# A chunked recurrent block on TensorE: shared operands in matmuls of 128 columns, and diagonal pairs as 128x128 weights

## The reference, cut to what matters

```python
def step(state, inp):
    r_t, w_t, k_t, v_t, a_t, b_t = inp
    sa = jnp.einsum('bhij,bhj->bhi', state, a_t)
    state = (state * w_t[:, :, None, :] + sa[..., None] * b_t[:, :, None, :]
             + v_t[..., None] * k_t[:, :, None, :])
    return state, jnp.einsum('bhij,bhj->bhi', state, r_t)
xs = tuple(jnp.moveaxis(t, 1, 0) for t in (r, decay, k, v, a_vec, b_vec))
_, ys = lax.scan(step, jnp.zeros((B, H, N, N), jnp.float32), xs)
```

## Time and profile before

| what | value |
|---|---|
| three runs | 1958.47, 1959.4 and 1967.14 us, median 1959.4 |
| span of the profiled execution | 1958.9 us |
| PE busy | 1641.4 us, 84% of the span |
| VectorE, ScalarE, POOL busy | 676.9, 370.8, 195.1 us |
| DMA | 537.14 MB, mean 274 GB/s |

### The profile page before, as it was taken

One profiled execution on the slowest core, in us unless ns is written; L12 is line 12 of the kernel. 1 busy time (PEld: TensorE's weight loads), 2 busy tenths in 40 slices (PEclk: granted clock), 3 DMA queues, 4 the chain that ended last, 5 costly groups with the idle time before them and its releaser, 6 DMA issues.

```text
span 1958.9 us, 30727 instructions
## 1 busy us (share of the span) xinstructions
PE 1641.4 (84%) x13306; PEld 1041.2 (53%) x13306; DVE 676.9 (35%) x1148; ACT 370.8 (19%) x746; POOL 195.1 (10%) x91
## 2 busy tenths in 40 slices
PE   9999999999999998766676787999988768666664
PEld 8998977997985854222122332867854223221221
DVE  1565421564531365111111124573365211111103
ACT  1444101444201251000000011331211000000001
POOL 2331422331420000000000000000300000000000
PEclk9999999999999999888878898999999989888888
DMA  9342444351453448999999997222156999999994
GB/s 383 106 165 97 162 159 172 100 171 44 190 213 156 172 185 351 427 427 427 427 427 427 425 388 315 105 86 72 64 238 281 427 426 425 426 428 427 427 427 192
DMA packets 48231, 537.14 MB, mean 274 GB/s; under 512 B 4533, under 2 KB 12981, under 8 KB 15033
## 3 DMA queue, kind: packets, MB, share of 16 engines
q1 hardware_dynamic: 46752, 528.27, 65.9%
q10 hardware_dynamic: 1304, 6.51, 0.9%
HBM read 533.71 MB, written 1.05 MB: 273 GB/s over the span
## 4 chain that ended last, share of the span: by engine, by line
PE 59%; DMA 31%; DVE 5%; ACT 3%; issue 1%; POOL 0%; DVEq 0%; ACTq 0%; POOLq 0%
PE ps L448 47%; DMA arena<-in_moe_w_gu 23%; PE ps L460 8%; DMA arena<-in_moe_w_down 6%; PE ps L466 2%; DMA ring<-in_moe_w_gu 2%; DVE x L1539 1%; ACT arena L2421 1%; DVE arena L1528 1%; ACT arena L2425 1%; DVE arena L1533 1%; DVE arena L1539 1%; ACT L2421 0%; DVE hb L1528 0%; DVE small L1543 0%
## 5 line engine op out<-in xcount | busy, mean ns | idle before, releaser
L460 PE MATMUL ps<-arena 128*32 128x512 f32 (+1 forms) x1348 | 201.6, 680 | 86.0 <-DMA arena<-in_moe_w_gu 66.4
L448 PE MATMUL ps<-hT,ring 128*128 128x256 f32 (+2 forms) x1600 | 265.5, 326 | 0.0
L2425 ACT ACTIVATE arena<-ps 128x512 f32<-128x512 f32 (+4 forms) x152 | 92.4, 608 | 898.8 <-PE ps L460 491.5
L460 PE MATMUL ps<-ring,arena 128*32 128x512 f32 x1248 | 178.6, 703 | 89.9 <-DMA ring<-in_moe_w_gu 71.9
L448 PEld LDWEIGHTS ps<-hT,ring 128*128 128x128 f32 (+1 forms) x1600 | 236.4, 186 | 25.1 <-issue 2.1
L1528 DVE TENSOR_TENSOR arena<-arena,ps 128x256 f32<-128x256 f32 (+3 forms) x110 | 55.6, 506 | 486.5 <-ACT arena L2421 432.8
L448 PE MATMUL ps<-arena 64*64 64x64 f32 (+11 forms) x2000 | 149.7, 302 | 30.8 <-ACT arena L2714 22.3
L460 PEld LDWEIGHTS ps<-arena 128*32 128x32 f32 (+1 forms) x1348 | 48.8, 124 | 221.6 <-DMA arena<-in_moe_w_gu 98.2
L460 PEld LDWEIGHTS ps<-ring,arena 128*32 128x32 f32 x1248 | 38.2, 120 | 205.2 <-DMA ring<-in_moe_w_gu 102.1
L448 PEld LDWEIGHTS ps<-arena 64*64 64x64 f32 (+4 forms) x2000 | 92.2, 150 | 86.4 <-ACT arena L2714 49.5
L448 PE MATMUL ps<-arena,ring 128*128 128x256 f32 (+2 forms) x928 | 129.6, 315 | 2.8 <-ACT hT L2425 1.4
(11 more groups left out here) (205 smaller groups left out, 1824.5 us busy)
## 6 DMA issues: line engine op xcount, KB each, us to landing
arena<-in_moe_w_gu SPq DMA_DIRECT2D x57, 2048.0 KB, 40.9
ring<-in_moe_w_gu SPq DMA_DIRECT2D x49, 2048.0 KB, 41.2
ring<-in_moe_w_down SPq DMA_DIRECT2D x35, 2048.0 KB, 41.3
arena<-in_moe_w_down SPq DMA_DIRECT2D x29, 2048.0 KB, 40.7
extra<-in_moe_w_gu SPq DMA_DIRECT2D x22, 2048.0 KB, 41.5
ring<-in_w_merge SPq DMA_DIRECT2D x16, 2048.0 KB, 8.3
ring<-in_w_in SPq DMA_DIRECT2D x9, 2048.0 KB, 7.3
ring<-in_attn_w_qkv SPq DMA_DIRECT2D x6, 2048.0 KB, 7.7
```

Source lines behind the costliest of these rows:

```text
L448: i = t.matmul(o, l, r, start=first, stop=last, skip_group_check=True)
L460: i = t.matmul(o, l, r, start=first, stop=last, skip_group_check=True)
L2425: s.activation(o, a, ACT.Copy).then_inc(*act.one(name))
```

## The change

`with_both` takes the place of four `pair` calls per block: the operands r and a lie beside each other (`r.ra`), so one matmul of 128 columns with b as weights gives rb and N, and one with k gives rk and ak. Its results fill two PSUM tiles, one for each partition half of the operands. U and W come from one matmul of 128 columns (`mv atok` holds both right sides), in two half tiles `UW0` and `UW1`; H and R likewise (`rb btok`), one tile for each chunk. The six Horner updates use weights of 128x128, with chunk 0's matrix in the upper left quarter, chunk 1's in the lower right and zeros elsewhere: 16 matmuls of 128x128 by 64 columns instead of 32 of 64x64 by 64 columns. To lay the weights so, ScalarE copies the first eight heads of pw1 and of Q twice, scaled by 1 and 0 over the partitions (`first_half`), and VectorE writes the other eight in one operation (`other_half`). `mv`, `ktok` and `btok` are moved between the updates. Memory is dealt out anew.

```diff
+    r.ra = arena[:, OWN + 4096:OWN + 8192].rearrange("p (t k s) -> p t k s", t=2, k=KT)
...
-        def quads(i, n, lhs, rhs, out, order=None):
+        def with_both(i, n, lhs):
             name = f"rw{i} {n}"
+            p = [tile(f"{name}{a}", (dve, f"{name}{a} out")) for a in range(2)]
+            mm([(p[a][64 * c:64 * c + 64, P * k:P * k + P], lhs[64 * a:64 * a + 64, k, i * P + 64 * c:i * P + 64 * c + 64],
+                 r.ra[64 * a:64 * a + 64, :, k, i * P + 64 * c:i * P + 64 * c + 64], True, True)
+                for k in range(KT) for c in range(2) for a in range(2)], name)
...
+        def step(n, rhs, last, power=None):
+            for i in range(NT):
...
+                mm([(p[:, 64 * b:64 * b + 64], B[i]["P"][:, P * b:P * b + P], B[i][rhs][:, 64 * b:64 * b + 64], True, True)
+                    for b in range(16)], name)
...
-        def summed(left, n, step):
-            for i in range(NT):
-                if step > 1:
-                    t.wait_ge(*dve(f"rw{i} {n}{step - 1} out"))
-                quads(i, f"{n}{step}", B[i][left], B[i]["X" if step > 1 else "Y"], dve)
...
-            pair(i, "N", r.bT, r.aa)
+            with_both(i, "N", r.bT)
             pair(i, "D", r.aa, r.bT)
-        values(1)
+            if i == 0:
+                values(1)
...
-        summed("d", "R", 1)
-        for i in range(NT):
-            pair(i, "rb", r.bT, r.rT)
-        summed("d", "R", 2)
-        for i in range(NT):
-            pair(i, "rk", r.kT, r.rT)
-        summed("d", "R", 3)
+        values_of_keys(0)
+        step("R1", "Y", "inv1", "pw1")
+        with_both(1, "K", r.kT)
+        step("R2", "X", "R1")
+        values_of_keys(1)
+        step("R3", "X", "R2")
+        t.wait_ge(*act("rw0 mv out"))
+        tokens(0, "ktok", r.kT)
...
+        t.wait_ge(*act("rw1 mv out"))
+        tokens(1, "ktok", r.kT)
+        step("P1", "Y", "R3", "Q")
+        tokens(0, "btok", r.bT)
+        step("P2", "X", "P1")
+        tokens(1, "btok", r.bT)
+        step("P3", "X", "P2")
...
-            quads(i, "U", B[i]["Y"], B[i]["mv"], act, (at_, lambda u: u, lambda u: u))
...
+                mm([(p[64 * c:64 * c + 64, P * (u % 8):P * (u % 8) + P], blk_of(B[i]["Y"], c, at_(u)),
+                     B[i]["mv atok"][64 * c:64 * c + 64, u], True, True) for u in range(8 * j, 8 * j + 8) for c in range(2)], name)
...
-            mm([(p[onto(u, c)], blk_of(d["W"], c, u), blk_of(d["btok"], c, u), True, True) for u, c in uc], name)
+            for n, c in ((c + 1, c) for c in range(2)):
+                w = 64 if i and c else P
+                mm([(p[c][64 * (u % 2):64 * (u % 2) + 64, P * (u // 2):P * (u // 2) + w], blk_of(d["W"], c, u),
+                     d["rb btok"][64 * c:64 * c + 64, 0:w // 64, 64 * u:64 * u + 64], True, True) for u in range(16)], f"rw{i} RH{c}")
...
+        def inverse_starts(i):
...
+            v.wait_ge(*pe(f"rw{i} N"))
+            for a in range(2):
+                masked(heads(d["n"], a), half_of(i, "N", a, 1), "m16", f"rw{i} n" if a else None)
+            v.wait_ge(*pe(f"rw{i} D"))
+            masked(u3(d["d"]), u3(ps(f"rw{i} D")), "n16", f"rw{i} D out")
+            for a in range(2):
+                masked(heads(d["Dm"], a), half_of(i, "N", a, 1), "mof")
+                masked(rb[:, a], half_of(i, "N", a, 0), "mle", f"rw{i} N{a} out")
...
+        def other_half(i, n):
+            v.wait_ge(*pe(f"rw{i} {n}"))
+            tt(B[i]["full"][:, 8:16], bc(u3(ps(f"rw{i} {n}"))[:, 8:16].unsqueeze(2), [P, 8, 2, 64]),
+               bc(tab["hnd"].unsqueeze(1).unsqueeze(3), [P, 8, 2, 64]), MUL, f"rw{i} {n} other")
...
+        def first_half(i, n):
+            s.wait_ge(*pe(f"rw{i} {n}"))
+            for c in range(2):
+                fn(B[i]["full"][:, 0:8, c], u3(ps(f"rw{i} {n}"))[:, 0:8], ACT.Copy, f"rw{i} {n} out" if c else None, scale=m.tab["hnd"][:, c:c + 1])
...
-    for q, step in enumerate(("rw1 ak", "rw1 mv", "rw1 rb", "rw1 rk")):
+    for q, step in enumerate(("rw0 K", "rw0 mv", "rw1 K", "rw1 mv")):
```

More of the change, by code:

```diff
@@ L430, in memory @@
     r.bT, r.aa = r.aT, r.kk
+    r.ra = arena[:, OWN + 4096:OWN + 8192].rearrange("p (t k s) -> p t k s", t=2, k=KT)
+    r.rb_btok = [arena[:, o:o + 2048].rearrange("p (t x) -> p t x", t=2) for o in (OWN + 2048, OWN + 13312)]
     r.add = [flat(r.kT)[:, 1024 * i:1024 * i + 1024] for i in range(NT)]
@@ L1359, in rwkv @@
             t.wait_ge(*dve(f"rw{i} D out"))
-            quads(i, "sq n", B[i]["d"], B[i]["n"], act)
-            quads(i, "sq d", B[i]["n"], B[i]["d"], act)
-        for i in range(NT):
-            pair(i, "ak", r.kT, r.aa)
+            quads(i, "sq n", B[i]["d"], B[i]["n"], (act, f"rw{i} sq n out"))
+            quads(i, "sq d", B[i]["n"], B[i]["d"], (act, f"rw{i} sq d out"))
+        with_both(0, "K", r.kT)
         for i in range(NT):
@@ L1366, in rwkv @@
             t.wait_ge(*pool(f"rw{i} Y"))
-            quads(i, "inv1", B[i]["d"], B[i]["Y"], dve)
-            quads(i, "pw1", B[i]["n"], B[i]["d"], act)
+            quads(i, "inv1", B[i]["d"], B[i]["Y"], (dve, f"rw{i} inv1 out"))
+            quads(i, "pw1", B[i]["n"], B[i]["d"], (act, f"rw{i} pw1 out"), (dve, f"rw{i} pw1 other"))
         t.wait_ge(*act("rw v1"))
-        for i in range(NT):
[L1371 to L1375, removed]
-        summed("d", "R", 1)
-        for i in range(NT):
-            pair(i, "rb", r.bT, r.rT)
-        summed("d", "R", 2)
-        for i in range(NT):
-            pair(i, "rk", r.kT, r.rT)
-        summed("d", "R", 3)
-        for i in range(NT):
-            t.wait_ge(*act(f"rw{i} mv out"))
-            tokens(i, "ktok", r.kT)
+        values_of_keys(0)
[6 more added lines that the diff above has]
+        tokens(0, "ktok", r.kT)
         for i in range(NT):
@@ L1392, in rwkv @@
             t.wait_ge(*act(f"rw{i} X0 out"))
[L1393 to L1400, removed]
+            quads(i, "Q", B[i]["Dm"], B[i]["X"], (act, f"rw{i} Q out"), (dve, f"rw{i} Q other"))
+        t.wait_ge(*act("rw1 mv out"))
[5 more added lines that the diff above has]
+        step("P3", "X", "P2")
         for i in range(NT):
             t.wait_ge(*dve(f"rw{i} P3 out"))
-            t.wait_ge(*act(f"rw{i} btok"))
-            quads(i, "U", B[i]["Y"], B[i]["mv"], act, (at_, lambda u: u, lambda u: u))
[L1405 to L1408, removed]
+            t.wait_ge(*act(f"rw{i} atok"))
+            for j in range(2):
+                name = f"rw{i} UW{j}"
+                p = tile(name, (act, f"rw{i} UW{j} a"), (dve, f"rw{i} UW{j} b"))
+                mm([(p[64 * c:64 * c + 64, P * (u % 8):P * (u % 8) + P], blk_of(B[i]["Y"], c, at_(u)),
+                     B[i]["mv atok"][64 * c:64 * c + 64, u], True, True) for u in range(8 * j, 8 * j + 8) for c in range(2)], name)
         def onto(u, c):
@@ L1472, in rwkv @@
         scan(1)
-        reads(1)
         scan(2)
@@ L1502, in blocks @@
         slot = m.ring[m.spare[i]]
[L1503 to L1506, removed]
+        d = {"P": slot[:, 0:2048], "Dm": slot[:, 2048:3072], "rk": slot[:, 3072:4096], "Q": flat(m.mT if i else r.Lc),
+             "rb": r.own[3 * i], "btok": r.own[3 * i + 1], "ak": r.own[3 * i + 2], "rb btok": r.rb_btok[i],
+             "mv atok": (flat(m.hT) if i else m.hb.rearrange("p t d -> p (t d)")).rearrange("p (u t n) -> p u t n", u=16, t=2)}
+        for pair, names in (("P", "nd"), ("Q", "YX")):
             for k in range(2):
                 d[names[k]] = d[pair][:, 1024 * k:1024 * k + 1024]
-        d["U"], d["W"], d["H"], d["G"] = d["n"], d["d"], d["E"], d["X"]
-        d["atok"], d["btok"], d["ktok"] = d["Nm"], d["Dm"], d["ak"]
+        d["UW"] = d["P"].rearrange("p (t u n) -> p t u n", t=2, u=16)
+        d["full"] = d["P"].rearrange("p (b c n) -> p b c n", b=16, c=2)
+        d["U"], d["W"], d["H"], d["G"] = d["n"], d["d"], d["Dm"], d["X"]
+        d["ktok"] = d["ak"]
         B.append(d)
@@ L2305, in rwkv @@
            ps("rw bonT")[:, 0:512].rearrange("p (g q n) -> p g q n", g=4, q=4)[:, :, :, 0:2], "rw bonT")
-        for i in range(NT):
-            masked(i, "ak", ("ak", "mlt"))
+        keys_read(0)
         for i in range(NT):
@@ L2367, in reads @@
         def reads(i):
[L2369 to L2371 removed]
+            for c in range(2):
+                v.wait_ge(*pe(f"rw{i} RH{c}"))
+                rt = rT[:, :, i * P + 64 * c:i * P + 64 * c + 64]
+                tt(rt, rt, read_or_gained(i, c, 0), ADD, f"rw{i} R{c}")
         def seen(i, rows):
@@ L2871, in rwkv @@
             out(i, "sq d", B[i]["d"])
+        def first_half(i, n):
+            s.wait_ge(*pe(f"rw{i} {n}"))
+            for c in range(2):
+                fn(B[i]["full"][:, 0:8, c], u3(ps(f"rw{i} {n}"))[:, 0:8], ACT.Copy, f"rw{i} {n} out" if c else None, scale=m.tab["hnd"][:, c:c + 1])
         for i in range(NT):
-            out(i, "pw1", B[i]["d"])
+            first_half(i, "pw1")
         for i in range(NT):
-            out(i, "mv", B[i]["mv"])
-        for i in range(NT):
-            out(i, "ktok", B[i]["ktok"], "")
```

(13 more changed lines are left out.)

97 lines of the change are left out of this document (57 added, 40 removed).

## The result

The changed kernel takes 1977.14 us, the median of five runs from 1973.44 to 1979.52, beside 1959.4 for the kernel before, also of five. The ratio of the two is 1.0077 (95% interval 1.0057 to 1.0097): slower, by more than the half per cent that can be told from no change. The profiled execution has a span of 1976.0 us, 17.1 more than before.

The account below looks back on a forecast made before the run. PE's in-order list was taken to bound the block, its growth delaying the DMA-bound weight stream and the end one for one. Terms summed to +17.2 us on 1958.9, giving 1976.1, as median 1976.5; eight-in-ten range 1967 to 1985.5 us.

Parts of the forecast that it names:

- U with W: Four merged half tiles of 32 records at 1.95 us each against 4 x 1.87: +0.3 us; range -3.7 to +7.8.
- Horner steps: Twelve R and P updates with full 128x128 weights cost 3.62 us each instead of 1.87: +21.0 us.
- rival that the load hides: Horner steps: weight load hides behind the matmul ahead, a step costs 1.87 us; about 1955.5 us; chance 0.12.
- Stops that go: PE's nine unexplained issue stops in the block, 10.0 us with restarts, mostly vanish as streams slow: -9.0 us.
- rival by which they stay: PE's stops in the block come from instruction supply and remain: +9.0 us more, about 1985.5 us; chance 0.10.
- Merged pair products: N with rb, ak with rk: eight products become four of 128 columns at 1.95 us: -0.3 us.
- rival of two at a time: Merged pair products overlap by two instead of four, 3.9 us each: +7.5 us, about 1984 us; chance 0.10.
- H with R: Merged per chunk, only two array quarters work instead of four: 6.8 us against 4.0, +2.8 us.
- The wait for a PSUM tile: Block 1's first squaring waits for VectorE to free one of N's two PSUM tiles: +2.7 us.
- The ScalarE wait: PE's wait ahead of P1 goes, since block 1's `ktok` fills it and VectorE takes half of Q: -1.2 us.
- The scan's cover: Block 1's R no longer stands between scan1 and the VectorE wait, leaving 1.6 us bare for 1.34: +0.3 us.
- rival that it absorbs it: After the block, the expert weight stream absorbs the block's delay: 1959.5 us; chance 0.04.

Follow-up runs that it names:

- e1: Changed kernel with its twelve Horner products back to 32 matmuls of 64x64 by 64 columns, all else kept; 1956.18 us, ratio to before 0.9984.
- e2: Changed kernel with each Horner matmul cut into two of 32 moving columns, same 128x128 weights, so twice the loads; 2092.72 us (one run).
- e3: Changed kernel with each Horner matmul cut by output into two with weights of 128 rows by 64 columns; 1957.9 us, ratio 0.9995.
- e4: Kernel before, with the matmuls inside each pair product reordered so that two quarters of the array work at a time, not four; 1970.35 us (one run).
- e7: Changed kernel with Horner products back on quarters and VectorE and scan reordered to shorten both new PE waits; 1953.55 us, ratio to before 0.9972.
- e5: Changed kernel with VectorE reordered to finish each half of N at once and free its PSUM tile early; 1971.02 us, ratio 1.0062.
- e6: Changed kernel with scan1 ahead of block 1's G as cover, and VectorE reading R before writing the state; 1973.16 us, ratio 1.0064.

## Why the prediction held

The forecast of 1976.5 us is 0.6 off the median, and the main term is shown: e1, e2 and e3 settle that a full-array step is paid for by its weight loads. Some terms beside it missed and cancelled: that the sum came within 1 us is luck, that it lies near 17 us isn't. (Two slips in it hardly matter: 1976.1 + 0.5 is 1976.6, and U with W without overlap would be +8.1, not +7.8.)

- **Horner steps**, predicted +21.0: twelve take 43.15 us from start to start, less 12 x 1.87 = +20.7. The 0.6 for switches between full-array and quarter products isn't seen apart from it; taken together it was 21.6 for 20.7. The rival that the load hides is refuted by the profile after, and e1 undoes the loss.
- **Stops that go**, predicted -9.0: 0.6 us are left, with the restart 0.8, so -9.2. The size was right, the reason only in part. The prediction laid the stops to the 16 ns rate alone and gave instruction supply to the rival by which they stay. But e4's pair products at 25 ns leave 6.3 us of them, and e7's squarings, which run at 29 ns a record, have a stop of 1.49 us. The traces put every stop at a block of PE's own instruction list (last section): supply is the cause they point to, and a slower list is why the stops went. e1 says which part did it: with steps in quarters 1.9 us are left, so most went with the merged products.
- **Merged pair products**, predicted -0.3: 1.83 us (2.84 to the transposes less 1.01 for D) for each N, 1.91 and 1.86 for the two of K, 7.43 for 8.08: -0.65. The rival of two at a time would have read 3.9 each.
- **U with W**, predicted +0.3: 6.82 us (1423.24 to 1430.06) for 4 x 1.87: -0.7. **H with R**, predicted +2.8: 2.91 (1430.06 to 1432.97) and 2.14, together 5.05 for 4.0: +1.1. Both terms were mis-sized by the same step: I took 0.122 us for two matmul records that share the array, from a row of four side by side; 6.82 us over 64 such pairs is 0.107, and 2.91 us over the 32 pairs of block 0's H with R is 0.091.
- **The wait for a PSUM tile**, predicted +2.7: 2.89, and e5 shows its cause. **The ScalarE wait** ahead of P1 is gone, -1.2 as predicted.
- **The scan's cover**, predicted +0.3: the wait is 2.37 for 1.34, +1.0. I took 1.6 us, VectorE's two operations with hand-overs. I missed that scan2 takes the PSUM tile of RH0, which VectorE reads only behind the state, from 1447.32 on and for 0.7 us; PE goes on at 1448.06, and the profile names that read (`arena`) as the releaser and not the state (`cz`). In e6, where the read comes first, the wait is 0.79.
- **The clock**, not in the sum: the squarings take 8.92 us where four products of 1.87 make 7.48 (+1.4), and the scan with the last chunk product about 1.5 us more than in e1 and e5. The windows say 0.81 and 0.61. The prediction took 1.00 for the whole block, as before.

20.7 - 9.2 - 0.65 - 0.7 + 1.1 + 2.9 - 1.2 + 1.0 + 2.9 = +16.85, beside the measured 16.94. Of the errors, the clock and the scan are 3.6 us that the sum lacked; U, W, H and R are 2.7 that it had too many, the switches, pairs and steps the rest.

The stream behind the block took the delay as predicted; the rival that it absorbs it is refuted by its first chunk at 1454.53. The prediction gave near 1456; the block began 1.2 us earlier than before.

## What to carry to other kernels

Two 64x64 weight matrices laid as one block-diagonal 128x128 halve the instructions and double the time where few columns move: the halves can no longer be loaded beside each other. Before packing, look in the trace for the packed shape at the same column count and read its start-to-start distance; counting instructions would have given the wrong sign here. Merging products that share the weights is sound, but look at how many PSUM tiles a merged product holds, and what has to be read before each comes back.

## What was not expected of the hardware

The granted clock fell behind waits of 2.4 and 2.9 us in some executions and not in others: 0.81 or 1.00 over the squarings, 0.61, 0.69 (in e3, 1425.35 to 1430.00) or 1.00 over the scan, with the same wait ahead. In e4 it was 0.50 from 1431.86 to 1435.28 us, behind a stop of 1.93 us. It fell to 0.50 inside e2's steps, in which PE was busy all the time but moved only 32 columns a load; the steps of 64 columns stayed at 1.00.

PE's stops without a releaser, up to 1.9 us each, keep their places from one execution to the next. The list of waits names nothing for them, but the trace does show what happens there. Its queue q8 moves instructions in transfers of 16 KB, and their number follows PE's matmul records: 115 and 116 for 13306 records, 112 for 12826, 109 for 12442. The pages, before and after:

```profile
q8 instruction: 115, 1.88, 0.4%
```

```profile
q8 instruction: 109, 1.79, 0.4%
```

In all ten runs together the block has 39 such stops. From one to the next there are 126 to 128 records, or a multiple of that, and every stop ends 1.20 to 1.60 us after a q8 transfer has landed. One example is the stop of 1.10 us before: a transfer runs from 1368.69 to 1370.12 us, and PE goes on at 1371.48. Where two stops follow each other by one transfer, 3.47 to 4.02 us lie between them, 27 to 32 ns a record; with transposes in between it was 6.1 to 6.9 us. So PE seems to outrun its own instruction list: pair products at 15.8 ns a record do so readily, quarter products at 29 ns now and then, and full-array steps at 113 ns leave the list time to get ahead. No run here changes the supply, so this is read from the traces and not tested.

The stops sum to 0.2 us in e3, 0.6 in the changed kernel and in e2, 1.1 in e6, 1.9 in e1, 2.4 in e5, 3.9 in e7, 6.3 in e4 and 8.5 to 9.3 in the kernel before. What sets when a transfer starts stays open: e1 and e3 issue equally many records at nearly the same rate, and differ by 1.7 us.
